# A hybrid attention encoder on one core: finer splits of the first weights, a whole probability product in the A heads, and three reorderings

## The reference

```python
h = _rmsnorm(x, norm_g[layer])
proj = h @ w_in[layer]                       # 2048 x 10304
aq, ak, av, ag, cq, ckv, kr, bg, mg = jnp.split(proj, SPLIT_POINTS, axis=-1)
# branch A, 8 heads: differential attention
s1 = qb1 @ k1 * scale + bias;  s2 = qb2 @ k2 * scale + bias
p = softmax(s1) - lam * softmax(s2)
oa = p @ v                                   # per head: 512 x 512 times 512 x 128
ya = (rmsnorm(oa) * silu(ag)) @ w_oa
# branch B, 8 heads: latent attention with a rotary part
q = _rmsnorm(cq) @ w_uq;  kv = _rmsnorm(ckv) @ w_ukv
ob = softmax(q_nope @ k_nope + q_rope @ k_rope) @ vb
yb = (ob * silu(bg)) @ w_ob
merged = sigmoid(ga) * ya + sigmoid(gb) * yb
x = x + merged @ w_out;  return _rmsnorm(x, final_g)
```

## Time and profile before

| | |
|---|---|
| median of 3 runs | 1426.17 us (1425.03 to 1426.52) |
| profiled execution | 1425.88 us, of which the traced span is 1424.1 us |
| PE busy | 1409.7 us (99%), 6604 matmuls |
| DVE busy | 1020.1 us (72%) |
| ACT busy | 706.9 us (50%) |
| granted TensorE clock | 0.999 of full speed |

### The profile page before, as it was taken

How to read it: one execution, slowest core, us unless ns; L and a number is a source line. 1 busy time by engine, 2 the same in 40 slices (tenths; PEclk the granted TensorE clock), 3 DMA queues, 4 the chain that set the end, 5 groups by cost and what they waited for, 6 DMA issues and landing times.

```text
span 1424.1 us, 17881 instructions
## 1 busy us (share of the span) xinstructions
PE 1409.7 (99%) x6604; PEld 1175.9 (83%) x6604; DVE 1020.1 (72%) x1381; ACT 706.9 (50%) x894; POOL 32.0 (2%) x52
## 2 busy tenths in 40 slices
PE   8999999999999999999999999999999999999997
PEld 7887888888888888888888888888888888888886
DVE  6967888898888868677667665666676354388966
ACT  6546334544344456665666667555564122224434
POOL 0000000000000000000000000000000000000000
PEclk9999999999999999999999999999999999999999
DMA  8449576766756542222222434322342444617674
GB/s 300 146 126 317 176 260 193 232 218 205 246 183 209 186 142 84 80 82 81 81 82 84 114 112 127 88 67 66 85 136 75 156 127 145 207 45 250 201 251 170
DMA packets 182976, 218.43 MB, mean 153 GB/s; under 512 B 19456, under 2 KB 133248, under 8 KB 182272
## 3 DMA queue, kind: packets, MB, share of 16 engines
q1 hardware_dynamic: 174304, 197.64, 44.7%
q10 hardware_dynamic: 8608, 19.93, 3.6%
HBM read 195.51 MB, written 22.02 MB: 153 GB/s over the span
## 4 chain that ended last, share of the span: by engine, by line
PE 91%; DVE 4%; DMA 2%; SPq 1%; ACT 1%; issue 1%; POOL 0%; POOLq 0%; DVEq 0%
PE duo L2118 28%; PE duo L2120 27%; PE duo L2119 27%; PE duo L2171 2%; DMA start_y<-start_columns 1%; PE duo L2148 1%; PE duo L2145 1%; DMA m_raw<-in_w_in_dram 1%; SPq L612 1%; DVE o_lo L1504 1%; PE duo L2162 1%; PE duo L2167 1%; PE duo L2163 1%; PE duo L2166 1%; PE duo L2164 1%
## 5 line engine op out<-in xcount | busy, mean ns | idle before, releaser
L1387 DVE TENSOR_TENSOR w_lo<-w_raw,w_hi 128x1024 fp32r<-128x1024 f32 (+1 forms) x116 | 135.3, 1167 | 100.1 <-ACT w_hi L783 99.5
L2118 PE MATMUL duo<-h_hi,w_hi 128*128 128x512 f32 x512 | 202.3, 395 | 0.0
L2120 PE MATMUL duo<-h_hi,w_lo 128*128 128x512 f32 x512 | 199.7, 390 | 0.0
L2119 PE MATMUL duo<-h_lo,w_hi 128*128 128x512 f32 x512 | 199.6, 390 | 0.0
L888 ACT ACTIVATE m_hi<-m_raw 128x2048 fp32r<-128x2048 f32 (+1 forms) x66 | 115.5, 1752 | 146.8 <-PE duo L2120 75.0
L783 ACT ACTIVATE w_hi<-w_raw 128x1024 fp32r<-128x1024 f32 (+1 forms) x118 | 119.2, 1011 | 124.7 <-DMA w_raw<-in_w_ob_dram 66.0
L1504 DVE TENSOR_TENSOR m_lo<-m_raw,m_hi 128x2048 fp32r<-128x2048 f32 (+3 forms) x71 | 141.9, 2001 | 19.4 <-ACT m_hi L888 19.1
L2118 PE MATMUL duo<-m_hi,h_hi 128*128 128x512 f32 x368 | 143.9, 391 | 2.3 <-DVE m_lo L1504 1.4
L2120 PE MATMUL duo<-m_hi,h_lo 128*128 128x512 f32 x368 | 143.2, 389 | 0.0
L2118 PE MATMUL duo<-m_hi,s_hi 128*128 128x512 f32 x320 | 124.5, 389 | 0.0
L2120 PE MATMUL duo<-m_hi,s_lo 128*128 128x512 f32 x320 | 124.5, 389 | 0.0
(11 more groups left out here) (322 smaller groups left out, 2969.6 us busy)
## 6 DMA issues: line engine op xcount, KB each, us to landing
m_raw<-in_w_in_dram SPq DMA_DIRECT2D x110, 512.0 KB, 4.6
w_raw<-in_w_in_dram SPq DMA_DIRECT2D x132, 256.0 KB, 3.0
o_raw<-in_w_out_dram SPq DMA_DIRECT2D x32, 512.0 KB, 5.0
spare<-in_w_in_dram SPq DMA_DIRECT2D x17, 512.0 KB, 4.8
h_raw<-in_w_in_dram SPq DMA_DIRECT2D x17, 512.0 KB, 5.0
w_raw<-in_w_oa_dram SPq DMA_DIRECT2D x32, 256.0 KB, 3.4
sig<-gates SPq DMA_DIRECT2D x8, 1024.0 KB, 6.2
w_raw<-in_w_ob_dram SPq DMA_DIRECT2D x32, 256.0 KB, 3.4
```

What stands on the lines that cost most here:

```text
L1387: dve.tensor_tensor(w_lo[:, piece.slot, 0:cols], w_raw[:, piece.slot, 0:cols], w_hi[:, piece.slot, 0:cols].bitcast(F32), ALU.subtract).the ...
L2118: pe.matmul(dst, lhs_hi, rhs_hi, start=start, stop=False)
L2119: pe.matmul(dst, lhs_hi, rhs_lo, start=False, stop=False)
L2120: return pe.matmul(dst, lhs_lo, rhs_hi, start=False, stop=stop)
```

## The change

1. **Opening.** ACT waits for the gains first. The high part of weight step 0 is made block by block (`first_hi`, 512 columns: block 0, then block 1) with the first unit of h between them by k (`first_unit_hi(0)`, `(1)`), then unit 1, then the other half of step 0; DVE follows in the same order (`first_unit_lo`). Weight step 1 is split in halves on both engines, and PE has waits for each part inside `values`.
2. **A heads.** The product with the values is one group of 12 matmuls of 512 columns at q = 7 (`pv_a`); the pair product at q = 4 is gone. High and low parts get whole buffers (`pt_hi_whole`, `pt_lo_whole`), and ACT no longer waits for the first pair. In step s = 2 the turn of tile 2 stands after five k blocks in place of four. Head 1's DVE waits once more, for two stores of gates whose space the low buffer takes. `pv_done` counts one per A head, so waits on it have new numbers.
3. **Three orders.** `LOW_FIRST` gains `V_STEPS + 1` (step 13) and `MID_SPLIT + 2`. In head 0 of branch B the piece split at s = 2 comes behind the low part of the rotary query.

```diff
-LOW_FIRST = [V_STEPS] + FIRST_END[:M_GROUPS] + SECOND_END[:M_GROUPS - 1]
-LOW_FIRST += [OUT0 + L_STEPS + i for i in (0, 1, 2, 4)] + [MID_SPLIT]
+LOW_FIRST = [V_STEPS, V_STEPS + 1] + FIRST_END[:M_GROUPS] + SECOND_END[:M_GROUPS - 1]
+LOW_FIRST += [OUT0 + L_STEPS + i for i in (0, 1, 2, 4)] + [MID_SPLIT, MID_SPLIT + 2]
+TURN_2_STEP = 2
-HALVED = (0, 3)
+HALVED = (0, 1, 3)
+SPLIT_HIS = (0, 0, 1, 3)
+        pt_hi_whole = at("pt_hi_whole", 182, [P, TOK, SEQ], F32R)
+        pt_lo_whole = at("pt_lo_whole", 152, [P, TOK, SEQ], F32R)
...
+            def first_hi(part):
+                st = MERGE[0]
+                act.wait_ge(m_in[st.raw], st.landed)
+                act.activation(hi_of(st, part, part + 1), raw_of(st, part, part + 1), ACT.Copy).then_inc(m_hi_ready, 1)
...
-            half_hi(0, 0)
             act.wait_ge(g_in_in, 16)
-            unit_hi(0)
+            first_hi(0)
+            first_unit_hi(0)
+            first_unit_hi(1)
+            first_hi(1)
+            unit_hi(1)
             half_hi(0, 1)
-            for i in range(1, 3):
-                unit_hi(i)
-            merge_hi(1)
+            unit_hi(2)
+            half_hi(1, 0)
+            half_hi(1, 1)
...
-                    if s or prev:
+                    if s not in (0, 2) or prev:
                         split_lo(Piece(B0 + s + AHEAD, h, B_STEPS), HALF_PIECE if half else 2 * HALF_PIECE)
                     b_step(s, h, pair, True, prev)
-                    if not s and not prev:
+                    if s in (0, 2) and not prev:
                         split_lo(Piece(B0 + s + AHEAD, h, B_STEPS), HALF_PIECE if half else 2 * HALF_PIECE)
...
+            def pv_a(head):
+                if not isinstance(head, int) or head > 0:
+                    pe.wait_ge(o_copied, head)
+                pe.wait_ge(pt_lo_ready, tile_no(head, TOK - 1))
+                pe.wait_ge(v_lo_ready, head + 1)
+                for k in range(TOK):
+                    last = three(OB[:, :], v_hl[:, 0, k, :], v_hl[:, 1, k, :],
+                                 pt_hi_whole[:, k, :], pt_lo_whole[:, k, :], k == 0, k == TOK - 1)
+                last.then_inc(pv_done, 1)
...
                 if q == 4 and prev:
-                    pv(h - 1, 0, True)
                     turn_p_a(h - 1, 2)
                 if q == 6 and prev:
                     turn_p_a(h - 1, 3)
                 if q == 7 and prev:
-                    pv(h - 1, 1, True)
+                    pv_a(h - 1)
...
-                            lambda: a_extras(2 * s, h, True, prev))
+                            lambda: a_extras(2 * s, h, True, prev), 5 if prev and s == TURN_2_STEP else 4)
```

More of the change, by code:

```diff
@@ L172 @@
 GATED_ORDER = [head for step in sorted(GATED_AT) for head in GATED_AT[step]]
-HALVED = (0, 3)
+HALVED = (0, 1, 3)
+SPLIT_HIS = (0, 0, 1, 3)
 def his_by(n):
-    return n + 1 + sum(s <= n for s in HALVED)
+    return n + 1 + sum(s <= n for s in SPLIT_HIS)
 WARM_UP, WARM_UP_TURN = 20, 2
@@ L790, in proj_split_hi, with pt_hi_a @@
                 act.activation(dst, src, ACT.Copy).then_inc(proj_hi, 1)
+            def pt_hi_a(head, t):
+                act.wait_ge(p_turned, tile_no(head, t))
+                act.activation(pt_hi_whole[:, :, t * P:(t + 1) * P],
+                               TR[:, :].rearrange("p (k c) -> p k c", k=TOK), ACT.Copy).then_inc(pt_hi_ready, 1)
             def pt_hi(head, t, src):
@@ L794, in pt_hi @@
                 if t >= 2:
-                    act.wait_ge(pv_done, head * 2 + 1)
+                    act.wait_ge(pv_done, head * 2 + (1 - HEADS))
                 act.activation(pt[:, 0, :, (t % 2) * P:(t % 2 + 1) * P],
@@ L822, in v_hi_a @@
                 if not isinstance(head, int) or head > 0:
-                    act.wait_ge(pv_done, head * 2)
+                    act.wait_ge(pv_done, head)
                 act.activation(v_hl[:, 0, :, :], v_raw[:, :, :], ACT.Copy).then_inc(v_hi_ready, 1)
@@ L1673, in _ @@
             dve.wait_ge(g_in_in, 16)
[L1674 to L1677, removed]
+            for j in range(2):
+                dve.wait_ge(m_hi_ready, j + 1)
+                part_lo(MERGE[0], j, j + 1, m_lo_first)
+                first_unit_lo(j)
             unit_lo(1)
-            dve.wait_ge(m_hi_ready, 2)
-            part_lo(MERGE[0], 2, 4, m_lo_ready)
+            dve.wait_ge(m_hi_ready, his_by(0))
+            part_lo(MERGE[0], 2, 3, m_lo_first)
+            part_lo(MERGE[0], 3, 4, m_lo_ready)
             unit_lo(2)
-            merge_lo(1)
+            dve.wait_ge(m_hi_ready, his_by(1) - 1)
+            part_lo(MERGE[1], 0, 2, m_lo_first)
+            dve.wait_ge(m_hi_ready, his_by(1))
+            part_lo(MERGE[1], 2, 4, m_lo_ready)
             for i in range(3, EARLY_UNITS):
@@ L1777, in a_step @@
                 if s == 1 and prev:
-                    pt_lo(h - 1, 0, TR)
+                    if first:
+                        for out_n in (g12_out, g22_out):
+                            dve.wait_ge(out_n, 16 * M_GROUPS)
+                    pt_lo_a(h - 1, 0)
                     max_a(h - 1, 2, first)
-                    pt_lo(h - 1, 1, TR)
+                    pt_lo_a(h - 1, 1)
                     if not cur:
@@ L2123, in tile, with project @@
                 return w_hi[:, piece.slot, c0:c0 + width], w_lo[:, piece.slot, c0:c0 + width]
-            def project(piece, dst, half, halves, rhs_hi, rhs_lo, k0, midway=None):
+            def project(piece, dst, half, halves, rhs_hi, rhs_lo, k0, midway=None, midway_at=4):
                 pe.wait_ge(lo_ready, piece.after(0))
                 for k in range(8):
-                    if k == 4 and midway:
+                    if k == midway_at and midway:
                         midway()
@@ L2184, in turn_p_b, with pv @@
                 turn(e_b[:, t % 2, :], SC[t], p_turned)
-            def pv(head, pair, in_a=False):
-                if in_a and pair == 0 and (not isinstance(head, int) or head > 0):
+            def pv_a(head):
+                if not isinstance(head, int) or head > 0:
                     pe.wait_ge(o_copied, head)
+                pe.wait_ge(pt_lo_ready, tile_no(head, TOK - 1))
[4 more added lines that the diff above has]
+                last.then_inc(pv_done, 1)
+            def pv(head, pair):
                 pe.wait_ge(pt_lo_ready, tile_no(head, 2 * pair + 1))
```

65 lines of the change are left out of this document (45 added, 20 removed).

## The result

| | before | with the change |
|---|---|---|
| median | 1425.88 us (18 runs, 1424.49 to 1427.62) | 1428.76 us (18 runs, 1426.81 to 1429.58) |
| ratio | | 1.0021, 95% interval 1.0014 to 1.0027 |
| traced span | 1424.1 us | 1426.3 us |

The account below looks back on a forecast made before the run. PE, busy 99% of the span, was taken as the bound. From 1425.88 us, gains of 3.2 and A-head losses of 3.0 gave 1425.7, or 1426.0 as a median (0.29 more); range 1422.4 to 1428.5, called the same.

Parts of the forecast that it names:

- The four gains: Opening 1.0, merge step 14 1.2, B head 0 0.6 and output weight 0.4: PE's waits there go, 3.2 us won.
- The opening: Start of the kernel: PE starts as before and weight step 1 no longer waits, gain 1.0, bounds 0.4 and 1.1.
- Heads 1 to 6: A heads 1 to 6: each pays 0.3 waiting at turn 3 for 0.15 saved by wider matmuls; 0.8 lost in all.
- And DVE cannot be earlier: A heads, ahead of turn 3: DVE works in one row from 623.17, its only idle time, 0.90, spent on ACT.
- Head 0: A head 0, with rotary angles on DVE: PE also waits 0.6 more for tile 3's low part; 0.9 lost.
- Head 7 is the dear one: A head 7: product starts at 840.30 behind DVE's low part, then PE has 2.73 in place of 1.44; 1.3 lost.
- The changed counts cost nothing: A heads: the changed counts, DVE's added wait on gate stores and ACT's dropped wait were said to cost nothing.
- The third rival: A heads: tile 3's low part late in every head, 0.9 per loop head, 1.3 in head 7; 1430.6 us, chance 0.05.
- the prediction's signs of being wrong: Turn 3 does not wait, an A head's period falls below that of before, or a new wait at step 2 or 15.

Follow-up runs that it names:

- experiment 1: Changed kernel with the A heads' product again in two pairs as before, leaving the opening and the three orders: 1422.96 us, ratio 0.9981 to the kernel before.
- experiment 4: Changed kernel with DVE's normalization of tile 3 ahead of the split of weight in A heads 0 to 6: 1425.79 us, ratio 1.0002 to the kernel before.
- experiment 3: Changed kernel with ACT's high part of head 7's turned tile 3 ahead of the split of the late weight piece: 1427.53 us, ratio 1.0012 to before.
- experiment 6: Changed kernel with the load of the next weight piece held back on SP until turn 3 of head 7: 1428.63 us, ratio 1.0019 to before.
- experiment 9: Changed kernel with 14 full-size and 28 small warm-up matmuls in place of 20 full-size on PE: 1427.84 us, ratio 1.0015 to before.
- experiment 11: Changed kernel with new orders in C steps and heads 0 to 6, rotary tables later, warm-up of 14 full-size and 28 small matmuls: 1422.23 us, ratio 0.9977 to before.

## Why the prediction was wrong

- *The four gains, 3.2.* Right: 0.7 + 1.26 + 0.6 + 0.5 = 3.1 in the trace, 2.5 to 2.7 in experiment 1. The opening gave 0.7 in place of 1.0: in that execution the gains landed 0.3 later than the working took, and ACT's start now hangs on them (in experiment 1 PE starts at 15.11).
- *Heads 1 to 6, 0.8.* Right in mechanism (turn 3 waits for the low part of tile 2, listed 0.17), a little small: 0.18 a head where the working has 0.15 (six heads of 0.15 make 0.9; the sum took 0.8). "And DVE cannot be earlier" holds for the order as written only: experiment 4 took the wait away with another order and left the 0.16 that the wider matmuls save.
- *Head 0, 0.9.* Right: 0.87, with the wait of 0.38 ahead of the product.
- *"Head 7 is the dear one ... 1.3 lost."* This step failed. The longer product cost the 1.3 that it names. But the working ended at "DVE's low part of tile 3 (839.55 + 0.69 = 840.24)", as if DVE's order alone set that time. ACT's high part of tile 3 stood behind the split of the piece, which began at 837.98 when the piece had just landed; the high part ended at 838.95 + 0.58 = 839.53, and DVE took it up at 839.55. There was nothing to spare, and so no wait that a view would list. The change made the transfer 1.2 longer, and the product started 1.2 later (experiment 3). Nor did the working look behind the product: the fourth store grew by 1.2 to 2.1, which cost PE 0.3 in the profile and about 1.0 in repeats, and the normalization of the result, which stands behind the stores in the same row of ACT, added a wait of 0.2. Together 3.4 in the profile (1.3 ahead of the product's start, 1.3 in it, 0.8 behind it) and some 0.7 more in the medians.
- *"The changed counts cost nothing."* True of the waits. But the missing matmuls also shorten PE's code, and where a piece of that code is loaded moved onto the two transfers (experiments 6, 9 and 11). No row of the trace before shows this as a cost, since there the packets fell between.

The third rival had the right sign and the wrong place: no loop head but head 0, which the forecast had priced, lost 0.9, and head 7 lost more than its 1.3. None of the prediction's signs of being wrong came: turn 3 waits, the A heads got longer, and no wait stands at step 2 or 15. Head 7's product even starts straight behind DVE (840.71 + 0.69 = 841.40), as was said; but DVE itself had waited 1.2 for ACT.

What stays open is what sets the moment of a code load. In experiment 9 the second packet of this stretch moved by 8 to 9 us against PE's work and the first by under 1; in experiment 11, with the same warm-up, both moved, by 6 and 7.

## What to carry to other kernels

Follow a removed piece of work past the place where it stood to the next transfer that someone waits for: here it was a landing with nothing to spare on ACT, an engine that was 50% busy. When the program of an engine gets longer or shorter, look in the DMA view for its instruction packets and on whose transfer they fall now. And where an engine's row looks full, try another order of it before calling it the bound: one exchange put the 0.9 us to use for which DVE stood idle in each of the heads 1 to 6, and PE gained 0.34 a head (41.71 to 41.37).

## What the runs showed of the hardware

A packet of PE's code, 0.02 MB, kept one of the 16 DMA engines busy for 0.9 to 2.0 us where it fell on the piece or the fourth store, and these ended 1.2 to 2.5 us later (the piece 5.5 to 5.6 against 6.7 to 6.9, the store 2.0 to 2.5 against 3.7 to 4.6), though by the rates 15 engines were done. The Trainium skill (Runtime: NRT & Kernel Launch, section Instruction fetch mechanics) says that an engine's code comes in blocks of 16 KiB by a DMA queue of its own and that the cost of crossing a block is "mostly hidden". The trace agrees on the block (41 packets, 0.67 MB) and on the queue (q8). Hidden it was for PE's own instructions, whose list of waits has none that goes with a packet, but not for the transfers beside it. The piece and the store counted as landed when the last trickle was in (860.9 for the bulk of the store, 862.2 for the trickle, 862.8 for ACT's start), and that is where these times come from.
